# A hybrid trunk's MoE gate moves from the summed tokens to the expert rows, with a wait on the last fetch ahead of the next panels

## What is computed

```python
for i in range(DEPTH):                                   # 4 layers
    mp = _adaln(c_ctx, w_ada[i], b_ada[i])               # six vectors for context tokens
    ms = _adaln(c, w_ada[i], b_ada[i])                   # six vectors for latent tokens
    ...                                                  # norm, mixer i % 3, gated sum
    hp = _modulate(_rmsnorm(xp, norm2[i]), mp[3], mp[4])
    hs = _modulate(_rmsnorm(xs, norm2[i]), ms[3], ms[4])
    xp = xp + mp[5] * _moe(hp, ...)                      # mp[5], ms[5]: the MoE gate
    xs = xs + ms[5] * _moe(hs, ...)

# _moe: two experts e per token, with shares w of the router
hg = t @ w_gate[e]; hu = t @ w_up[e]                     # 1024 -> 256
y += w[e] * ((silu(hg) * hu) @ w_down[e])                # 256 -> 1024
```

## Time and profile before

| | us |
|---|---|
| median of 3 runs | 1914.71 (1910.42 to 1921.96) |
| profiled execution, its own time | 1922.27 |
| its span in the profile | 1920.5 |
| PE busy | 1536.9 (80%) |
| DVE busy | 521.4 (27%) |
| ACT busy | 431.7 (22%) |
| POOL busy | 130.9 (7%) |
| DMA, mean over the span | 227 GB/s |
| POOL L1856, idle ahead of it | 657.7, four times, on the stored rows |
| ACT L1795, idle ahead of it | 77.2, twelve times, on the fetches |
| DVE L1467, idle ahead of it | 90.8, ten times, on ACT L1795 |
| PE L508 (norm), idle ahead of it | 130.9, eight times, on ACT |

### The profile page before, as it was taken

The page is one execution under the profiler, slowest core; times in us unless marked ns, Lnnn a source line. Parts: engine busy times, 40 slices in busy tenths (PEclk is TensorE's granted clock), DMA queues, the critical chain, the costliest instruction groups (busy, mean ns, idle before and its releaser), DMA issues. The chain is left out here.

```text
span 1920.5 us, 19165 instructions
## 1 busy us (share of the span) xinstructions
PE 1536.9 (80%) x7307; PEld 847.4 (44%) x7307; DVE 521.4 (27%) x1292; ACT 431.7 (22%) x836; POOL 130.9 (7%) x114
## 2 busy tenths in 40 slices
PE   2897878889926799389999999886998498969942
PEld 1445444444405544155555555434443346444411
DVE  0142210252125621232112221104320355062203
ACT  0213320222224311252111111003121306032201
POOL 0000000110022100200000000002000100110002
PEclk9898988889968899799999999997999699979976
DMA  6877897759981499825444445053898621049983
GB/s 190 292 252 268 283 313 242 255 209 413 411 313 56 160 390 410 313 66 161 154 142 145 157 146 169 1 218 132 308 411 330 267 88 50 0 146 393 411 320 110
DMA packets 205371, 436.72 MB, mean 227 GB/s; under 512 B 19008, under 2 KB 124256, under 8 KB 205152
## 3 DMA queue, kind: packets, MB, share of 16 engines
q1 hardware_dynamic: 179504, 392.75, 56.1%
q10 hardware_dynamic: 22320, 30.20, 4.5%
q0 software_dynamic: 3456, 12.58, 1.7%
HBM read 409.80 MB, written 25.69 MB: 227 GB/s over the span
## 5 line engine op out<-in xcount | busy, mean ns | idle before, releaser
L885 PE MATMUL bank<-gate_up_weights,hT_gathered 128*64 128x512 f32 (+1 forms) x1280 | 259.2, 606 | 28.4 <-SPq L477 25.1
L753 PE MATMUL bank<-panel,hT 128*128 128x512 f32 x384 | 170.5, 598 | 0.7 <-ACT mod_bc L1582 0.7
L885 PEld LDWEIGHTS bank<-gate_up_weights,hT_gathered 128*64 128x64 f32 (+1 forms) x1280 | 84.5, 134 | 195.3 <-issue 190.6
L508 PE MATMUL bank<-const_base,xn 128*128 128x128 f32 x192 | 39.6, 397 | 130.9 <-ACT xn L1563 130.9
L899 PE MATMUL bank<-down_weights,actT 128*64 128x512 f32 (+1 forms) x640 | 138.6, 603 | 2.5 <-ACT actT L1761 2.5
L560 PE MATMUL bank<-panel,cond_columns 128*32 128x384 f32 x768 | 83.0, 555 | 56.0 <-DMA panel<-in_w_ada 28.7
L580 PE MATMUL bank<-panel,hT 128*128 128x512 f32 x288 | 126.1, 596 | 1.1 <-DVE hT L1079 1.1
L753 PEld LDWEIGHTS bank<-panel,hT 128*128 128x128 f32 x384 | 71.4, 190 | 90.8 <-issue 89.9
L870 PE MATMUL bank<-h_hi,P 128*128 128x512 f32 x216 | 96.3, 446 | 8.4 <-DVE P L1412 8.4
L508 PEld LDWEIGHTS bank<-const_base,xn 128*128 128x128 f32 x192 | 37.1, 214 | 135.8 <-issue 113.9
L1588 ACT ACTIVATE ada_panel_rows<-bank 128x384 f32<-128x384 f32 x64 | 31.4, 490 | 265.4 <-PE bank L560 150.2
(11 more groups left out here) (270 smaller groups left out, 1987.1 us busy)
## 6 DMA issues: line engine op xcount, KB each, us to landing
panel<-in_w_ada SPq DMA_DIRECT2D x64, 1536.0 KB
down_weights<-in_moe_w_down SPq DMA_DIRECT2D x74, 1024.0 KB, 15.4
gate_up_weights<-in_moe_w_gate SPq DMA_DIRECT2D x148, 512.0 KB, 13.4
gate_up_weights<-in_moe_w_up SPq DMA_DIRECT2D x148, 512.0 KB, 14.4
y_by_slot<-y_rows ACTq DMA_DIRECT2D x36, 512.0 KB, 7.1
panel<-in_ret_w_in SPq DMA_DIRECT2D x16, 1024.0 KB
panel<-in_attn_w_qkv SPq DMA_DIRECT2D x6, 2048.0 KB
panel<-in_attn_w_o SPq DMA_DIRECT2D x4, 2048.0 KB
```

Of the source, the lines that this page charges most:

```text
L508: last = PE.transpose(ps[k % 4][:, t * 128:(t + 1) * 128], xn[:, t, k * 128:(k + 1) * 128], ident)
L753: last = PE.matmul(ps[t][:], hT[:, k, t * 128:(t + 1) * 128], panel[f % 2][:, k, :], start=k == 0, stop=k == KD - 1)
L885: last = PE.matmul(ps[2][width * s:width * s + width, :], hg[:, j, k, width * s:width * s + width], gu_ring[w][:, :, k, :], start=k == 0, ...
```

## The change

The gate is no longer applied to the summed tokens. Each slot of a row belongs to a context or a latent token, and within an expert the context tokens come first, so one more product of ones with the assignment of tile 0 on PE gives the number of context tokens per expert (prompt). From it DVE makes a column `latent` of 0 and 1 per slot and row (in units for rows 0 to 7, in unit_prompts behind row 4 for row 8), and gdiff, the difference of the two gate vectors. In each row DVE forms the gate of every slot, `grow = gdiff * latent + gate`, and multiplies each half row by it as it leaves PSUM, where ACT copied it before. ACT still issues the store.

In the tail ACT's scale, the gate product and POOL's sums are gone. DVE adds each fetched tile, times its share, to x: two operations per tile, each behind its own fetch, for which every fetch has its own semaphore. And SP waits, ahead of the next mixer's panels, for the sixth fetch.

```diff
@@ sync: start of a layer
             if l:
                 sp.wait_ge(sem("experts_read"), l)
+                sp.wait_ge(sem(f"y_gathered{2 * TILES - 1}"), 16 * l)
@@ pe_route
-        last.then_inc(sem("ranks"), 1)
+        PE.matmul(ps[2][:, 64:80], ones[:], asg[:, 0, :], start=True, stop=True).then_inc(sem("ranks"), 1)
@@ dve units(l), at its end
+            for i in range(2):
+                o = slice(CAP * i, CAP * i + CAP)
+                V.tensor_tensor(latent[o, 0:PAIRS], in_cap[o, :].broadcast_to([CAP, PAIRS]),
+                                prompt[o, :].rearrange("p (r i) -> p i r", i=2)[:, i, :], ALU.is_ge)
+            step(V.tensor_tensor(gdiff[:], gate_bc[:, 1, :], gate_bc[:, 0, :], ALU.subtract))
+
+        def unit_prompts():
+
+            first, bound = rt[:, 600:600 + UNITS], rt[:, 428:428 + UNITS]
+            step(V.tensor_tensor(uprod, ue[:], prompt.unsqueeze(1).broadcast_to([128, UNITS, EXPERTS]), ALU.mult))
+            step(V.tensor_reduce(bound, uprod, AX.X, ALU.add))
+            step(V.tensor_tensor(bound, bound, first, ALU.subtract))
+            for i in range(4):
+                o = slice(SUB * i, SUB * i + SUB)
+                last = V.tensor_tensor(latent[o, PAIRS:ROWS], in_sub[o, :], bound[o, i:i + 1], ALU.is_ge)
+            step(last)
@@ dve row(l, q)
             if q < PAIRS:
                 row_gathered(l, q + 1)
-                row_turned(l, q + 1)
+            if rows_of(l, q):
+                dve.wait_ge(sem(f"y_stored{q % 2}"), 16 * rows_of(l, q))
+            step(V.scalar_tensor_tensor(grow[:], gdiff[:], latent[:, q:q + 1], gate_bc[:, 0, :], ALU.mult, ALU.add))
+            for half in range(2):
+                o = slice(half * 512, half * 512 + 512)
+                dve.wait_ge(sem("row_down"), 2 * n + half + 1)
+                V.tensor_tensor(ybuf[:, q % 2, o], ps[6 + half][:], grow[:, o], ALU.mult).then_inc(sem("row_y"), 1)
+                if half == 0 and q < PAIRS:
+                    row_turned(l, q + 1)
@@ dve combine(l)
             for t in range(TILES):
-                dve.wait_ge(sem("y_scaled"), TILES * l + t + 1)
-                step(V.scalar_tensor_tensor(ytok[:, 1, t, :], ytok[:, 1, t, :], rt[:, 406 + t:407 + t], ytok[:, 0, t, :],
-                                            ALU.mult, ALU.add))
-                term = V.tensor_tensor(ytok[:, 1, t, :], ytok[:, 1, t, :], gate_bc[:, COND[t], :], ALU.mult)
-                if t < TILES - 1:
-                    term.then_inc(sem("moe_term"), 1)
-                else:
-                    step(term)
-                    V.tensor_tensor(x[:, t, :], x[:, t, :], ytok[:, 1, t, :], ALU.add).then_inc(sem(f"moe_added{t}"), 1)
+                for a in range(2):
+                    dve.wait_ge(sem(f"y_gathered{2 * t + a}"), 16 * (l + 1))
+                    last = V.scalar_tensor_tensor(x[:, t, :], ytok[:, a, t, :], rt[:, 403 + 3 * a + t:404 + 3 * a + t], x[:, t, :],
+                                                  ALU.mult, ALU.add)
+                    if a == 0:
+                        step(last)
+                last.then_inc(sem(f"moe_added{t}"), 1)
@@ act row(l, q)
-            if rows_of(l, q):
-                e.wait_ge(sem(f"y_stored{par}"), 16 * rows_of(l, q))
-            for half in range(2):
-                e.wait_ge(sem("row_down"), 2 * n + half + 1)
-                S.activation(ybuf[:, par, half * 512:half * 512 + 512], ps[6 + half][:], ACT.Copy).then_inc(sem("row_y"), 1)
-                if half == 0 and q < PAIRS:
-                    row_turned(l, q + 1)
+            if q < PAIRS:
+                row_turned(l, q + 1)
             e.wait_ge(sem("row_y"), 2 * n + 2)
             e.dma_start(y_rows[SLOTS * q:SLOTS * q + SLOTS, :], ybuf[:, par, :]).then_inc(sem(f"y_stored{par}"), 16)
@@ act, tail: scale_rows is gone
-            scale_rows(l)
@@ pool combine(l)
             for t in range(TILES):
                 for a in range(2):
                     G.indirect_dma_start(ytok[:, a, t, :], None, y_rows[:],
-                                         bass.IndirectOffsetOnAxis(slot_of_token[:, a, t:t + 1], 0)).then_inc(sem(f"y_gathered{t}"), 16)
-            for t in range(TILES - 1):
-                pool.wait_ge(sem("moe_term"), (TILES - 1) * l + t + 1)
-                G.tensor_tensor(x[:, t, :], x[:, t, :], ytok[:, 1, t, :], ALU.add).then_inc(sem(f"moe_added{t}"), 1)
+                                         bass.IndirectOffsetOnAxis(slot_of_token[:, a, t:t + 1], 0))\
+                        .then_inc(sem(f"y_gathered{2 * t + a}"), 16)
```

More of the change, by code:

```diff
@@ L56, in shape_constants @@
     tie = np.broadcast_to(np.float32(4) - np.arange(4, dtype=np.float32), (128, 4))
+    places = np.stack([p % CAP, p % SUB], axis=1)
     caps = np.broadcast_to(4 * np.arange(1, QUADS, dtype=np.float32), (128, QUADS - 1))
@@ L65, in shape_constants @@
     base = np.concatenate([ident, tri, iota, sel, tie, caps, halfpow, quad, steps, lower, first,
-                           np.broadcast_to(slot0, (128, EXPERTS)), np.broadcast_to(past0, (128, EXPERTS))],
+                           np.broadcast_to(slot0, (128, EXPERTS)), np.broadcast_to(past0, (128, EXPERTS)), places],
                           axis=1).astype(np.float32)
@@ L121, in build_trunk @@
     mods = keep("mods", [48, 2])
-    kb = keep("const_base", [3 * 128 + 2 + 4 + QUADS - 1 + 64 + STEPS + EXPERTS * EXPERTS + UNITS + 2 * EXPERTS])
+    kb = keep("const_base", [3 * 128 + 2 + 4 + QUADS - 1 + 64 + STEPS + EXPERTS * EXPERTS + UNITS + 2 * EXPERTS + 2])
     vecs = keep("vector_rows", [3, 128])
@@ L135, in build_trunk @@
     slot_of_token = keep("slot_of_token", [2, TILES], I32)
+    latent = keep("latent_of_slot", [ROWS + 1])
     ones = keep("ones", [128])
@@ L190, in build_trunk @@
     (ytok,), _ = region(("y_of_token", [2, TILES, D]), start=mix0)
+    (gdiff, grow), _ = region(("gate_difference", [D]), ("gate_of_slot", [D]), start=mix0)
     uprod = lpart[:, 0:UNITS * EXPERTS].rearrange("p (u e) -> p u e", e=EXPERTS)
@@ L1320, in route @@
             step(V.tensor_scalar(rankm[:], rk16, -1.0, None, ALU.add))
-        counted, excl = rt[:, 480:544], rt[:, 544:560]
+        counted, excl, prompt = rt[:, 480:560], rt[:, 176:192], rt[:, 544:560]
         def units(l):
@@ L1453, in row @@
                 row_gathered(l, q + 1)
-                row_turned(l, q + 1)
+            if rows_of(l, q):
[7 more added lines that the diff above has]
+                    row_turned(l, q + 1)
         def more(n, p):
+            bound = rt[:, 428:428 + UNITS]
             atleast(dve, "o_gather", 2 * n)
@@ L1461, in more @@
             V.tensor_tensor(act[:], ps[2][:, FE:2 * FE], silu[:], ALU.mult).then_inc(sem("o_act"), 1)
+            for i in range(4):
+                o = slice(SUB * i, SUB * i + SUB)
+                V.tensor_tensor(latent[o, ROWS:ROWS + 1], in_sub[o, :], bound[o, ds(4 + 4 * p + i, 1)], ALU.is_ge)                    .then_inc(sem("o_latent"), 1)
+            atleast(dve, "o_latent", 4 * n + 4)
+            V.scalar_tensor_tensor(grow[:], gdiff[:], latent[:, ROWS:ROWS + 1], gate_bc[:, 0, :], ALU.mult, ALU.add)\
+                .then_inc(sem("o_gate"), 1)
+            atleast(dve, "o_gate", n + 1)
+            atleast(dve, "o_stored", 16 * n)
+            atleast(dve, "o_down", n + 1)
+            V.tensor_tensor(ybuf[:, 1, 0:512], ps[6][:], grow[:, 0:512], ALU.mult)
+            V.tensor_tensor(ybuf[:, 1, 512:1024], ps[7][:], grow[:, 512:1024], ALU.mult).then_inc(sem("o_y"), 1)
         def combine(l):
             for t in range(TILES):
-                dve.wait_ge(sem("y_scaled"), TILES * l + t + 1)
-                step(V.scalar_tensor_tensor(ytok[:, 1, t, :], ytok[:, 1, t, :], rt[:, 406 + t:407 + t], ytok[:, 0, t, :],
-                                            ALU.mult, ALU.add))
-                term = V.tensor_tensor(ytok[:, 1, t, :], ytok[:, 1, t, :], gate_bc[:, COND[t], :], ALU.mult)
-                if t < TILES - 1:
-                    term.then_inc(sem("moe_term"), 1)
-                else:
-                    step(term)
-                    V.tensor_tensor(x[:, t, :], x[:, t, :], ytok[:, 1, t, :], ALU.add).then_inc(sem(f"moe_added{t}"), 1)
+                for a in range(2):
[5 more added lines that the diff above has]
+                last.then_inc(sem(f"moe_added{t}"), 1)
         dve.wait_ge(sem("vT_ps"), 1)
@@ L1505, in _ @@
             row_place(l, 0)
-            step(V.tensor_copy(counted, ps[2][:, 0:64]))
+            step(V.tensor_copy(counted, ps[2][:, 0:80]))
             row_gathered(l, 0)
             row_turned(l, 0)
+            dve.wait_ge(sem("gate_bc"), 4 * (2 * l + 2))
+            dve.wait_ge(sem("mix_added"), 6 * (l + 1))
             units(l)
@@ L1783, in more @@
             S.activation(actT[:], ps[3][:, 0:256].rearrange("p (c s) -> p c s", c=2), ACT.Copy).then_inc(sem("o_actT_sb"), 1)
-            atleast(e, "o_down", n + 1)
-            S.activation(ybuf[:, 1, 0:512], ps[6][:], ACT.Copy)
```

(5 more changed lines are left out.)

9 lines of the change are left out of this document (5 added, 4 removed).

## The result

The changed kernel takes **1894.72 us** (median of 4 runs, 1889.39 to 1898.69) against 1917.48 us (4 runs, 1910.42 to 1921.96) on the same chip: a ratio of 0.9879, 95% interval 0.9848 to 0.9910. A second measurement gave 0.9900 (0.9884 to 0.9916).

A forecast was written before the change was run, and what follows sets the result against it. TensorE sets the pace except in the four layer-end tails and layer 3's DMA-bound last row; -21.8 - 19.3 + 0.5 + 5.0 + 1.6 = -34.0 us, set against the median 1914.71: 1881 us, range 1872 to 1893.

The forecast's parts named there:

- Tails: Ends of the four layers, first fetch to x: shorter additions and SP's wait together, forecast at -41.1 us.
- The wait: SP holds the next mixer's panels: the three inner tails land 12.50 us after the first fetch, saving 19.3 us.
- the additions: Tails: two DVE operations per tile, x done 1.4 us after the last landing, saving 21.8 us over four layers.
- Rivals 1 and 2: Tails: 1, additions hold off fetch issues, 1891 us, chance 0.11; 2, the wait speeds nothing up, 1900 us, chance 0.07.
- Product on DVE: Half rows leave PSUM by DVE product: 0.5 us lost at the layers' last rows, nothing at the 32 handovers.
- rival 3: Expert rows: DVE becomes the bound at the hT_gathered copy; chance 0.04 with gain left or none, 0.03 slower (1926 us).
- rival 4: Mixer start: a panel comes late, 5 us lost three times, 1896 us; chance 0.02.
- slower inner stores: Ahead of the inner tails: if inner stores behave like the last, 2.0 x 3 = 6 us are lost.
- Router: Ahead of the signal ranks: one more product of ones, 0.4 us a layer, 1.6 us in all.
- Row 0: units() gains comparisons and gdiff ahead of row 1's P: 1.1 or 1.4 us a layer, 5.0 us in all.
- Layers 0 and 3: Row 0 there: P is ready before TensorE comes, so 1.1 of the 1.4 us show.
- The wait, "at nothing": Loads queued behind SP's wait cost nothing: the norm hides it, with 9 us to spare.

The follow-up runs named there:

- e1: The changed kernel without SP's wait for the sixth fetch: 1913.19 us, ratio 0.9980 to the kernel before.
- e2: The kernel before with SP's wait alone, its old tail additions kept: 1905.96 us, ratio 0.9955 to the kernel before.
- e7: The changed kernel with all DVE tail additions held until the sixth fetch has landed: 1915.05 us (one run).
- e3: The changed kernel with gate_difference (gdiff) moved behind the first row's act: 1888.61 us (one run).
- e5: The changed kernel; SP also waits for small loads on ACT's queue before the next expert row and retention's modulation panels: 1888.29 us (one run).
- e6: The changed kernel with gdiff and comparisons behind row 0's act, prompt product behind signal ranks, SP waiting for small loads: 1880.29 us, ratio 0.9796 to before.
- e9: The kernel before with two unused DVE operations and DVE's two waits put ahead of row 1's P: 1932.56 us (one run).

## Why the prediction was wrong

- **Tails, right.** -40.1 against -41.1. The wait, measured by e1, gave 17.3 of 19.3; the additions gave the rest, 22.8 against 21.8. Landings in the inner tails came after 12.7 to 13.1 us instead of 12.50. x follows the last landing by one operation, as costed.
- **Rivals 1 and 2.** The second has fallen (e2). The first is real and small (e7). An issue lost up to 1.06 us, near the 1.3 of the rival, but the tails lost less. The first fetch landed after 4.4 us and not after the 5.5 that I had inferred, so two issues and not one are exposed.
- **Product on DVE, right.** Behind row 1's gate products the rows of layers 0 to 2 took 121.7, 121.5 and 121.7 us, before 121.2, 121.9 and 121.3; rival 3, with its 0.96 us behind the copy, did not come up. Neither did rival 4. The range also allowed for slower inner stores; from the last product to the first fetch they took 4.3 to 4.9 us, before 4.3 to 4.6.
- **Router, right.** One more product delays the first gather by 0.43 to 0.50 us in layers 1 to 3 (forecast 0.4).
- **Row 0, mis-sized, and here is most of the error.** This is the step that failed. The forecast took the pause for P as time lost once: 1.1 or 1.4 us a layer, 5.0 in all. The pause came: the earlier trace rows had 1.36, now 2.97, 1.6 longer (e3 puts 1.3 of it down to gate_difference and so 0.35 to the two comparisons). But behind it TensorE's clock fell, and the gather, the act transposes and all up to row 1's gate products took 9.50 instead of 7.92 us. From the first gather to row 1's gate products the four layers lost 3.0, 4.3, 2.8 and 2.7 us, 12.7 instead of 5.0. In layer 1, 1.6 is the pause, 1.6 the clock behind it, and 1.1 is row 0's own gather up to its gate products, which took 8.35 instead of 7.25 us at a lower granted clock (a mean of 0.64 instead of 0.79); that has no cause that I can show. In the second profile of the changed kernel layer 1 lost the same 4.3, but as 1.6 and 2.7: row 0 took 7.21 there and the stretch 10.64.
- **Layers 0 and 3** were costed from the earlier trace rows, where P was there before TensorE came for it. That was so because the first gate products ran at the lower clock, 8.79 us. In the changed kernel they took 7.09, TensorE came 1.7 us sooner, and so met the whole pause. (Granted clock: a mean of 0.80 from 408.5 to 417, and 1.00 from 397.8 to 404.8.) In the second profile they took 8.78 in layer 0, the pause was 1.27, no fall followed, and the layer lost 1.25 us, near the 1.1 of the forecast; all four lost 11.0 there. So the price was right for the case that the earlier trace rows show. The first gate products were slow in layers 0 and 3 in the profiles of before and of e2, and in 6 of 40 layers in the ten others; what decides it is not shown. Cover that consists of slow products is not to be counted on. Layer 0, the kernel before and the changed one:

```profile
408.43 8.79 PE L885 MATMUL bank<-gate_up_weights,hT_gathered 128*64 128x512 f32 x32 [0.83 <-ACT hT_gathered L1747]
417.14 0.50 PE L870 MATMUL bank<-h_hi,P 128*128 128x512 f32 x1
```
```profile
397.79 7.09 PE L890 MATMUL bank<-gate_up_weights,hT_gathered 128*64 128x512 f32 x32 [0.83 <-ACT hT_gathered L1787]
407.86 0.50 PE L875 MATMUL bank<-h_hi,P 128*128 128x512 f32 x1 [2.98 <-DVE P L1433]
```

- **The wait, "at nothing", the second step that failed.** The list of what is queued behind SP's wait was complete, but I asked only who waits for these loads, and not whom they meet at their new time. The pooling counts came 3.5 us later (e5). Mixer 1 took 3.8 us more. The kernels without this meeting (e1, e2, e5, e6, e9) still take 1.1 to 1.3 us more than the profile of before, e2 and e9 with the code of before in this place, so that part is not the change's.
- **Mixer 2** took 494.2 us against 492.3, but it lies between 490.5 and 495.1 over all kernels and follows none of the edits. I put it down to scatter.

Together: +1.0 (tails) + 5.3 (rows: 12.4 against 7.1, net of the 2 us by which layer 3's last store was faster, 3.80 instead of 5.76 us from the end of the last copy or product to the first fetch) + 5.3 (mixers) = 11.6, against the 11.2 us by which the medians on one chip (-22.8) missed the forecast (-34.0). The faster store is luck and not the change's: in e2, with the code of before, it was as fast, and in e9 it was slow again (4.41 and 6.07 us from TensorE's last product, before 6.43, changed 4.56). The other 2.8 us of the miss in absolute time are the kernel before, whose median moved from 1914.71 to 1917.48.

## What to carry to other kernels

Cost a pause of TensorE twice: its length, and the products behind it at half the clock where the pause is much longer than those that the trace shows without a fall. A pause alone behaved alike each time here, at 3 us and at up to 1.7 us; nothing between was measured at this place, and two close together did not behave alike. Work that is put ahead of a handover on DVE belongs behind the next one if its result is needed later; here that is a few moved lines, worth 12 to 16 us of 1895. And where a wait moves a block of loads, look for small loads on another queue in their new stretch: they take part of the bandwidth at the moment when someone on the path waits for them.

## What the runs showed of the hardware

- The fall can come after the pause. In layer 1 of the changed kernel the first five gather products behind it ran as fast as before (0.39 to 0.44 us, the first 0.50), and the slow ones follow from 651.26 to 654.25. In four of the 20 cases all twelve gather products were slow. The clock fell in all 20 cases; at which product differed.
- An issue of a fetch on POOL, behind the first of a tail, takes 0.94 us alone (e2, e7: 40 of 40). In all profiles 40 such issues took longer, 1.18 to 2.00 us. Each of them had begun while a DVE addition with all operands in SBUF (the engines' on-chip memory) was running that had started 0.10 to 0.92 us earlier, and each ended 0.81 us after that addition did. Where the addition started less than 0.1 us ahead of the issue or during it, the issue took 0.93 or 0.94 us (41 times), and the addition its 1.28 to 1.33.
- The head of the program, the same in all kernels, took between 359.8 and 370.8 us. That is 11 us of scatter ahead of the first changed line, and larger than most terms of the sum: one profile against another can't show a difference of this size unless the stages are compared one by one.
